# The next pair's projections issued ahead of the scores in TensorE's attention steps

## The reference

```python
c_q = _rmsnorm(p[..., :o1], g_q[l])                       # 384 wide
q = (c_q @ w_uq[l]).reshape(b, s, MLA_HEADS, 64 + 32)     # 8 heads
c_kv = _rmsnorm(p[..., o1:o2], g_kv[l])                   # 256 wide
kv = (c_kv @ w_ukv[l]).reshape(b, s, MLA_HEADS, 64 + 64)
k_nope, v = kv[..., :64], kv[..., 64:]
sc = einsum("bqhd,bkhd->bhqk", qn, k_nope) + einsum("bqhr,bkr->bhqk", qr, k_rope)
pr = softmax(sc * scale, axis=-1)
y_attn = einsum("bhqk,bkhd->bqhd", pr, v)
# beside it, on other columns of p: u = a * sigmoid(gt), a depthwise convolution of
# 31 taps over the positions, layer norm, silu; then [y_attn, u] @ w_o
```

## Time and profile before

| | |
|---|---|
| median of 3 runs | 2196.03 us (2195.57 to 2197.51) |
| the profiled execution, its own time | 2195.85 us |
| its span, first to last instruction | 2194.1 us |
| TensorE busy | 2010.7 us (92% of the span) |
| DVE, ACT, POOL busy | 1196.4, 965.7, 135.2 us |
| attention steps of layer 0 | 929.4 to 1083.3 us of the span |
| attention steps of layer 1 | 1613.6 to 1762.6 us |
| DMA | 162.31 MB, 24.6% of 16 engines' span |

### The profile page before, as it was taken

How to read it: one execution, slowest core, us unless ns; L and a number is a source line. 1 busy time by engine, 2 the same in 40 slices (tenths; PEclk the granted TensorE clock), 3 DMA queues, 4 the chain that set the end, 5 groups by cost and what they waited for, 6 DMA issues and landing times.

```text
span 2194.1 us, 26233 instructions
## 1 busy us (share of the span) xinstructions
PE 2010.7 (92%) x8419; PEld 1572.8 (72%) x8419; DVE 1196.4 (55%) x1956; ACT 965.7 (44%) x1729; POOL 135.2 (6%) x144
## 2 busy tenths in 40 slices
PE   7999889889999989977899999999978799999997
PEld 6777768668878867644487888787745477888786
DVE  4443356553333355846566666536766656666634
ACT  4554464343433333545454343434455544343432
POOL 0001100100000003200010000002120001000000
PEclk9999989999999999979999999999999999999999
DMA  3112113123322213201032333223210022333222
GB/s 127 49 62 67 62 33 100 54 84 98 96 91 96 96 53 81 42 13 29 29 91 88 100 91 103 89 97 85 63 23 17 29 68 87 101 91 104 90 98 82
DMA packets 158293, 162.31 MB, mean 74 GB/s; under 512 B 46328, under 2 KB 112846, under 8 KB 158220
## 3 DMA queue, kind: packets, MB, share of 16 engines
q1 hardware_dynamic: 158220, 161.38, 24.6%
HBM read 159.24 MB, written 2.10 MB: 74 GB/s over the span
## 4 chain that ended last, share of the span: by engine, by line
PE 80%; DVE 10%; ACT 7%; issue 2%; POOL 0%; DMA 0%; ACTq 0%; DVEq 0%; POOLq 0%
PE bank_a L1897 13%; PE bank_b L1897 12%; PE bank_b L1899 12%; PE bank_b L1898 12%; PE bank_a L1898 12%; PE bank_a L1899 12%; DVE arena L1241 3%; PE bank_b L2159 2%; PE bank_b L2257 2%; DVE w_lo L1238 1%; PE bank_a L1984 1%; DVE arena L1238 1%; ACT w_hi L952 1%; DVE x_t L1238 1%; DVE soft L1747 1%
## 5 line engine op out<-in xcount | busy, mean ns | idle before, releaser
L1238 DVE TENSOR_TENSOR w_lo<-w_raw,w_hi 128x512 fp32r<-128x512 f32 (+3 forms) x621 | 426.8, 695 | 766.1 <-ACT w_hi L952 442.3
L952 ACT ACTIVATE w_hi<-w_raw 128x512 fp32r<-128x512 f32 (+3 forms) x396 | 233.6, 600 | 453.0 <-PE bank_b L1899 230.5
L1897 PE MATMUL bank_b<-h_hi,w_hi 128*128 128x512 f32 x816 | 322.0, 395 | 4.4 <-DVE var L1256 3.9
L1897 PE MATMUL bank_a<-h_hi,w_hi 128*128 128x512 f32 x720 | 285.6, 397 | 40.5 <-DVE h_lo L1241 20.4
L1898 PE MATMUL bank_b<-h_lo,w_hi 128*128 128x512 f32 x816 | 318.8, 391 | 0.0
L1899 PE MATMUL bank_b<-h_hi,w_lo 128*128 128x512 f32 x816 | 318.6, 390 | 0.0
L730 ACT ACTIVATE w_hi<-w_raw 128x512 fp32r<-128x512 f32 x225 | 140.5, 630 | 326.3 <-PE bank_a L1899 179.8
L1898 PE MATMUL bank_a<-h_lo,w_hi 128*128 128x512 f32 x720 | 283.5, 394 | 0.0
L1899 PE MATMUL bank_a<-h_hi,w_lo 128*128 128x512 f32 x720 | 283.1, 393 | 0.0
L1241 DVE SCALAR_TENSOR_TENSOR arena<-arena,cols_all 128x512 f32<-128x512 f32 x350 | 244.2, 750 | 4.3 <-ACT arena L1076 4.3
L1897 PE MATMUL bank_b<-split,w_hi 128*128 128x512 f32 x436 | 176.9, 406 | 38.2 <-DVE w_lo L1238 20.8
(11 more groups left out here) (235 smaller groups left out, 2542.0 us busy)
## 6 DMA issues: line engine op xcount, KB each, us to landing
w_raw<-in_w_up_dram SPq DMA_DIRECT2D x240, 256.0 KB, 3.1
w_raw<-in_w_down_dram SPq DMA_DIRECT2D x152, 256.0 KB, 2.7
w_raw<-in_w_in_dram SPq DMA_DIRECT2D x64, 256.0 KB, 2.9
w_raw<-in_w_gate_dram SPq DMA_DIRECT2D x32, 256.0 KB, 2.8
w_raw<-in_w_o_dram SPq DMA_DIRECT2D x32, 256.0 KB, 2.7
w_raw<-in_w_out_dram SPq DMA_DIRECT2D x16, 256.0 KB, 2.7
w_raw<-in_w_in_dram SPq DMA_DIRECT2D x16, 192.0 KB, 2.3
w_raw<-in_w_in_dram SPq DMA_DIRECT2D x16, 144.0 KB, 2.1
```

The source lines that it names most:

```text
L952: nc.scalar.activation(w_hi[:, s, 0:c], w_raw[:, s, 0:c], ACT.Copy).then_inc(w_round, 1)
L1238: return nc.vector.tensor_tensor(out_, a, b, op)
L1897: nc.tensor.matmul(out_, a_hi, b_hi, start=start, stop=False, skip_group_check=loose)
```

## The change

In TensorE's queue `beside(i, m)` is put ahead of `scores2(g + 2)` in every step.

```diff
                 for g in range(BLOCKS + PV_LAG):
                     i, m = g // (2 * TT), g % (2 * TT)
+                    if i + 1 < PAIRS:
+                        beside(i, m)
                     if g + 2 < BLOCKS:
                         scores2(g + 2)
-                    if i + 1 < PAIRS:
-                        beside(i, m)
```

## The result

The changed kernel takes 2200.82 us (median of 20 runs, 2197.44 to 2210.39), the kernel before 2196.38 us (20 runs, 2195.43 to 2198.21). The ratio is 1.0021, 95% interval 1.0014 to 1.0028: 4.4 us slower, where 14.5 were forecast. The changed kernel's runs also spread over 13 us, those of before over 2.8.

The account below looks back on a forecast made before the run. It took a loop of waits through ACT's rounding, DVE's rest and TensorE's projection, values and transposes to bound the attention steps; 11.1 us at full clock plus 3.4 for the clock gave 14.5, so 2210.4 us, range 2202.5 to 2222.

Parts of the forecast that it names:

- The wait ahead of the projections stays, the scores move onto the loop: m = 1 to 3 of pairs 0 to 2: projections start as before; three scores matmuls delay the transposes by 0.70 us.
- Pairs 0 and 1: 6 x 0.70: m = 1 to 3, where ACT's copy waits for the transposes in six places: 4.2 us lost per layer.
- Pair 2's 1.36 us: m = 1 to 3 of pair 2, where ACT is later than the transposes: cost less slack, 1.36 us per layer.
- m = 0 at nothing: Steps m = 0, where keys go before scores: neither waits, both end before the values; cost nothing.
- The sum at the full clock, 11.1 us: Attention steps of both layers: 4.2 + 1.36 = 5.56 us per layer, none regained later, 11.1 us in all.
- The clock, +3.4 us: Pair 0's six query steps in both layers: scores at the half-level clock cost 0.56 us more each; bounds 0 and 3.4.
- low end of 2202: Low end of the forecast case: sum at full clock with layer 0 as warm as layer 1, 11.1 - 4.9 = 6.2.
- Colder: Rival: longer idle ahead of projections puts full-clock steps at the half level; 2217 to 2231 us, chance 0.15.
- Hidden anyway: Rival: ACT or DVE later in all nine steps, slack takes up the transposes' delay; 2196 to 2199 us, chance 0.06.
- Faster: Rival: projections fill the wait for the exponential at pair 0, m = 1, if `w_lo` is there; 2188 to 2193, chance 0.03.

Follow-up runs that it names:

- filled order of before: The kernel before, with extra matmuls of the scores' shape put into TensorE's idle time (113 a layer), nothing computed changed: 2180.18 us, ratio 0.9927.
- filled pair: The kernel before and the changed kernel, each with extra matmuls in TensorE's idle time (113 and 144 a layer): 2180.18 and 2191.16 us.
- bare pair of kernels: The kernel before and the changed kernel, both without extra matmuls: 2196.38 and 2200.82 us.
- early rounding: Against the kernel before, ACT rounds the query weights ahead of the step's exponential, not behind its copy of the transposes; TensorE's order unchanged: 2168.38 us, ratio 0.9876.

## Why the prediction was right or wrong

*The wait ahead of the projections stays, the scores move onto the loop.* Right. The nine waits went to 22.2 us (forecast 20 to 22), the turns to 5.96 and 5.09 us (5.96, 5.1).

*Pairs 0 and 1: 6 x 0.70.* Right in kind, too large at the full clock: 0.47 to 0.56 in pair 0 and at m = 1 of pair 1, 0.70 only at the last two. I took the six waits of ACT's copy in the earlier trace rows as a property of the loop. In layer 0 of the filled order of before only two of them are left, 0.83 and 0.55 us, both in pair 1; in pair 0 and at m = 1 of pair 1 the transposes are then done some 0.2 us before ACT is free, and the waits of the kernel before came from the half level. So those places have slack, as pair 2 has. Pair 2's 1.36 us: measured 1.35.

*m = 0 at nothing.* Right as the kernel ran: 0.1 us. With the clock held the traces show a gain of 0.6 us a layer.

*The sum at the full clock, 11.1 us.* The filled pair gave 11.0, but that close a match is partly luck: the turns add up to 9.6 us and the steps at the full clock to 8.4, and the rest of the 11.0 lies for the most part outside the steps.

*The clock, +3.4 us.* **This is the step that failed.** It says "the idle time ahead gets longer in all of them, so I take the upper end", and even its lower bound was 0. I priced only the scores, at the place where they come to stand, and only upward. In its place the medians of the filled and the bare pair of kernels put the term at 4.4 - 11.0 = -6.6 us, and the stretches of the traces at 14.6 - 18.9 = -4.3. I had counted only the six query steps of pair 0 as half-level ones, and read the clock as lowest there, 0.74. The kernel before was paying in other places already: its granted clock from 957.5 to 974.5 was 0.70, layer 0 ran S6 to Q9 at 0.82, 2.93 us longer than the changed kernel at 0.97, and it took 1.26 and 1.24 us longer from S21 to the end of the two layers' steps. After the change part of the half-level time lies behind the longer waits at Q9 and Q17 of layer 0 and Q3 of layer 1. The average stays at 0.87 in layer 0 and costs less where it falls now. The 4.9 us between the layers, which I had in hand from the earlier trace rows, showed how much such a shift is worth with no instruction changed; I used it for the range, as a low end of 2202, and not far enough.

*The rivals.* "Colder" came at single turns (Q17 of layer 0 at 0.78 for 1.00, Q3 of layer 1 at 0.73 for 1.00), but the average clock stayed within 0.01. "Hidden anyway" had the size nearly right and the cause wrong, since most of the transposes' delay was not taken up by slack but offset elsewhere. "Faster" had no footing; `w_lo` still came last.

What stays open: why the half level moved where it did, and why the stretches outside the steps differ by 1 to 2 us between executions. The runs show that filling idle time removes most of the half level; none of them says where it will fall.

## What to carry to other kernels

In a loop over several in-order queues, work that stands ahead of a wait can be free where the same work behind it is not; count the scores, copies or loads that a wait hides before moving anything past it, and look at what makes the wait: putting ACT's rounding in its own idle time was worth 28.8 us where the order on TensorE was worth 4 to 11. And when a change shifts TensorE's idle time, compare turns of the loop and the granted clock stretch by stretch, not totals: a total may hide more than half of the loss.

## What the runs showed of the hardware

I had not expected that idle TensorE is worth so much: 113 useless matmuls a layer took 16.6 us off the kernel, with the granted clock over the steps up from 0.87 and 0.92 to 0.98 and 0.99, and 86 took 9.5 us off the early rounding (0.92 and 0.93 before). The Trainium skill ("TensorE: Matmul & The Clock Gate", HAM oscillation) warns of idle gaps between bursts of matmuls; the trace agrees: behind the 3.11 us wait at Q9 the changed kernel ran at the half level, 0.66 over that turn. The traces also show that the share of half-level time alone does not give its cost: at 0.87 in both profiles, layer 0 took 0.56 us more after a change that put 4.8 us onto its loop, and from S21 on the lower clock, 0.82 for 0.89, went with the shorter time.
